# Softmax scales folded into the queries, maximum taken with its sign, relative bias added in place in the bank

## The chip, the core and the metric

The kernel runs on one core of a Trainium2 chip. The metric is the device time of one execution in microseconds, the median of several executions. The core has TensorE (PE: matmuls and transposes), VectorE (DVE), ScalarE (ACT), GpSimd (POOL) and SyncE (SP, which here only issues DMAs). The engines run their own instruction streams and meet at semaphores. Matmul results land in eight banks of PSUM.

## The reference, cut to what matters

Two transformer layers over 256 tokens and 256 context tokens, width 1024. Layer 0 has a gated spatial mixer and a differential attention (four heads, two maps each), then a dense feed-forward network. Layer 1 has a neighbourhood attention with a relative bias (eight heads), a latent attention (four heads), then a mixture of eight experts. The three attentions are what the change touches:

```python
# layer 0: two maps per head, scale = 1/sqrt(64), queries and keys after rope
s = einsum('bqhmd,bkhmd->bhmqk', q, k) * scale
p = einsum('bhmqk,m->bhqk', softmax(s), [1, -lam])
# layer 1, heads of kind C: scale_c = 1/sqrt(64); bias and mask on the 256 local keys only
s_loc = einsum('brqhd,brkhd->bhrqk', qg, kg) * scale_c + bias
s_ctx = einsum('brqhd,bkhd->bhrqk', qg, k_ctx) * scale_c
p = softmax(concatenate([s_loc, s_ctx]))
# layer 1, heads of kind D: scale_d = 1/sqrt(96), no bias
p = softmax(einsum('bqhd,bkhd->bhqk', q, k) * scale_d)
```

## The kernel before

Weights stream through a ring of six 1 MB buffers (`RAW`), each loaded by SP when the one six before it is released, and large matrix products are made of three matmuls over high and low halves. The work runs stage by stage: input products of layer 0 (`run("ev")`), first attention (`att0`), output product, feed-forward, input products of layer 1 (`run_od()`), second attention (`att1`), output product (`odo`), the experts, which fill the second half of the time. Each stage needs the results of the one before.

An attention is a list of units, each one head and 128 queries. `att0` has 16 units with two maps each, 256 keys in eight of them and 512 in the others. `att1` has 16 units of kind C with a bias, then 8 of kind D, all with 512 keys. Each of PE, ACT and DVE walks the list in its own loop, written out in `pe_attention`, `act_attention` and `dve_attention`; the order on an engine is fixed by these loops.

- PE, in step i (L697): scores of unit i+1 into bank 0 or 2 (L691; waits for `exp` of unit i-1), then the four transposes of unit i-1 (L706; wait for `prob` of unit i-1), then, in four steps, a share of the modulation products (`pe_mod_rows`, L571; `pe_mod_turn`, L579), then, for i odd, the product with the values for a pair of units (L717). So the transposes of an even unit are followed by L717, those of an odd unit are not.
- DVE, in step i (L754): the negative row maximum of unit i, then reciprocal (L789) and normalisation (L797, or L792 and L794 for two maps) of unit i-1, which increments `prob`; at odd steps also the low half of a finished pair (L807) or its copy (L804).
- ACT, in step i (L722): the exponentials of unit i with their row sums (L733; wait for `negmax` and for the transposes of unit i-2), the copy of the transposed unit i-1 (L743), at even steps of `att1` the high half of a pair (L750).

For a unit with a bias DVE first waits for the transposes of unit i-2 (L766), since the probabilities of that unit lie in the buffer it will write, and for the bias tile (L767). It then writes the scaled context half (L769) and the scaled local half plus bias (L771) into that SBUF buffer `PB`, and takes the maximum from there (L774). Without a bias, DVE takes the maximum from the bank (L778), waits for itself (`link`), and multiplies it by the scale (L781).

The bias tiles have two buffers. SP (`load_bias`, L941) loads each by two DMAs (L951) once the semaphore `biased` says that the unit two before has used the buffer; POOL then multiplies by the mask and adds the negative infinities (L991, L993) and increments `bias_ready`. The rest of SP's weight loads are queued behind these. The queries come out of the banks by ACT copies: L1033 (s 4 and 5 for layer 0), L1126 (kind C), L1105 (kind D).

Of the kernel before, what the change touches and what calls it, by code (L numbers as in the profile page):

```python
# [23 lines left out]
ALU = mybir.AluOpType  # L24
# [26 lines left out]
NSP_E = 3  # L51
CAP = 128
LAM_INIT = 0.8 - 0.6 * math.exp(-0.3 * 0)

# [109 lines left out]
def trunk(nc, w, out):  # L164
    ctx = ExitStack()
    with ctx:
# [486 lines left out]
        for h in range(4):  # L653
            for qb in range(4):
                nk = 2 if qb < 2 else 4
                att0.append(dict(
                    q=[QK[64 * m:64 * m + 64, h, P * qb:P * qb + P] for m in range(2)],
                    k=[QK[64 * m:64 * m + 64, 4 + h, 0:P * nk] for m in range(2)],
                    nk=nk, scale=1.0 / math.sqrt(64), bias=None, v=[V[:, kt, P * h:P * h + P] for kt in range(nk)],
                    o=slice(0, P), dst=(h, P * qb)))  # L660
        att1 = []
        for h in range(8):
            for qb in range(2):
                p0 = 64 * (h % 2)
                att1.append(dict(
                    q=[QC[p0:p0 + 64, h // 2, P * qb:P * qb + P]], k=[KC[p0:p0 + 64, h // 2, :]],
                    nk=4, scale=1.0 / math.sqrt(64), bias=(h, qb), v=[VCT[:, kt, 64 * h:64 * h + 64] for kt in range(4)],
                    o=slice(p0, p0 + 64), dst=(h // 2, 256 + P * qb)))
        for h in range(4):
            for qb in range(2):  # L670
                att1.append(dict(
                    q=[QD[0:96, h, P * qb:P * qb + P]], k=[KD[0:96, h, :]],
                    nk=4, scale=1.0 / math.sqrt(96), bias=None, v=[VD[:, kt, P * h:P * h + P] for kt in range(4)],
                    o=slice(0, P), dst=(4 + h, 256 + P * qb)))
# [46 lines left out]
        def act_attention(act, a, units, between=lambda i: None):  # L721
            for i in range(len(units) + 3):  # L722
                between(i)
                if i < len(units):
# [5 lines left out]
                    for m in range(len(u["q"])):  # L730
                        src = PB[:, 2 * (i % 2), :n] if u["bias"] else PS[2 * (i % 2) + m][:, :n]
                        c = 8 + 8 * (i % 2) + m
                        last = act.activation(PB[:, 2 * (i % 2) + m, :n], src, ACT.Exp, bias=SM[:, c:c + 1],  # L733
                                              scale=1.0 if u["bias"] else u["scale"],
                                              accum_out=SM[:, c + 2:c + 3])
# [16 lines left out]
        def dve_attention(dve, a, units, between=lambda i: None):  # L752
            lag = 3 + a
            for i in range(len(units) + lag):  # L754
                between(i)
                if i < len(units):
# [7 lines left out]
                    if u["bias"]:  # L764
                        if i >= 2:
                            dve.wait_ge(S(f"ptrans{a}"), i - 1)  # L766
                        dve.wait_ge(S("bias_ready"), i + 1)  # L767
                        b = PB[:, 2 * (i % 2), :]
                        dve.tensor_scalar(b[:, :CTX], PS[2 * (i % 2)][:, :CTX], u["scale"], None, ALU.mult)\  # L769
                           .then_inc(S("biased"), 1)  # L770
                        dve.scalar_tensor_tensor(b[:, CTX:], PS[2 * (i % 2)][:, CTX:], u["scale"], BT[:, i % 2, :],  # L771
                                                 ALU.mult, ALU.add).then_inc(S("biased"), 1)
                        dve.wait_ge(S("biased"), 2 * i + 2)
                        dve.tensor_reduce(SM[:, c:c + 1], b[:, :], AX, ALU.max, negate=True)\  # L774
                           .then_inc(S(f"negmax{a}"), 1)
                    else:
                        for m in range(len(u["q"])):
                            last = dve.tensor_reduce(SM[:, c + 6 + m:c + 7 + m], PS[2 * (i % 2) + m][:, :n], AX,  # L778
                                                     ALU.max, negate=True)
                        link(dve, last)  # L780
                        dve.tensor_scalar(SM[:, c:c + 2], SM[:, c + 6:c + 8], u["scale"], None, ALU.mult)\  # L781
                           .then_inc(S(f"negmax{a}"), 1)
                if 1 <= i <= len(units):
# [101 lines left out]
        def _(sp):  # L885
# [55 lines left out]
            def load_bias():  # L941
                sp.wait_ge(S("n4_hl"), KT)
                for i in range(NB_):
                    h, qb = att1[i]["bias"]
                    if i >= 2:
                        sp.wait_ge(S("biased"), 2 * i - 2)
                    for r in range(2):
# [49 lines left out]
        def _(act):  # L997
# [21 lines left out]
            for g, s in run("ev"):  # L1019
# [3 lines left out]
                for j in range(2):  # L1023
# [8 lines left out]
                    elif s < 8:  # L1032
                        act.activation(QK[:, 2 * (s - 4) + j, :], b[:, :], ACT.Copy).then_inc(S("ev_evac"), 1)  # L1033
                    else:
                        dst = V[:, 2 * j:2 * j + 2, 256 * (s - 8):256 * (s - 7)]
                        act.activation(dst, b[:, :].rearrange("p (t n) -> p t n", t=2), ACT.Copy)\
                           .then_inc(S("ev_evac"), 1)
# [61 lines left out]
            def act_latent(i0, i1):  # L1099

                for i in range(i0, i1):
                    act.wait_ge(S("mla_full"), i + 1)
                    b = PS[2 + i % 2]
                    if i < 4:
                        act.activation(QD[0:96, i, :], b[0:96, :SEQ], ACT.Copy).then_inc(S("mla_evac"), 1)  # L1105
                    elif i < 8:
# [4 lines left out]
            for g, p, s in run_od():  # L1111
# [10 lines left out]
                for j in range(2):  # L1122
                    act.wait_ge(*bank_full(g, j))
                    b = PS[2 + j] if s == 1 else PS[j]
                    if s < 2:
                        act.activation(QC[:, 2 * s + j, :], b[:, :SEQ], ACT.Copy).then_inc(S("od_evac"), 1)  # L1126
                    elif s < 4:
# [836 lines left out]
```

## Time and profile before

| | us |
|---|---|
| median of 3 executions | 2023.33 |
| lowest, highest | 2022.06, 2024.96 |
| the profiled execution | 2020.79 |
| its span in the trace | 2018.6 |
| PE busy | 1908.7 (95%) |
| DVE busy | 1278.3 (63%) |
| ACT busy | 1083.9 (54%) |
| POOL busy | 28.3 (1%) |
| first attention, from its first scores to its last pair | 194 to 245 |
| second attention, kind C | 831 to 893 |
| second attention, kind D | 893 to 917 |

Busy shares are averages over stages with different limits. The granted clock of PE is listed as a share of its higher level. Matmuls are pipelined and the ends in the trace are modelled, so an interval between two starts is safer than a duration. The chain of waits follows the work back from the last instruction, at each step to what released it; its pieces add up to the span.

### The profile page before, as it was taken

To read this page: it belongs to the slowest core of one execution; us is meant where nothing else is said; L and a number is where in the kernel's file an instruction comes from. 1 tells how busy PE (TensorE), PEld (TensorE's weight loads), DVE (VectorE), ACT (ScalarE), POOL (GpSimd) and SP (SyncE) were. 2 spreads that over 40 slices of the span, in tenths; PEclk is the share of its full clock that TensorE was granted. 3 is DMA by queue.
4 is the path that set the end of the run, shared out by engine and by line. 5 is a ranking of instruction groups with operands and counts; after the bars stand their busy time and mean duration, and the time that the engine had idled before them with its cause. 6 is when DMAs were issued, how large, how long until landed. Compare 5 with 4: busy or idle time off the path is not lost.

```text
span 2018.6 us, 23685 instructions
## 1 busy us (share of the span) xinstructions
PE 1908.7 (95%) x9802; PEld 1520.0 (75%) x9802; DVE 1278.3 (63%) x1219; ACT 1083.9 (54%) x1105; POOL 28.3 (1%) x44
## 2 busy tenths in 40 slices
PE   5998798999989989898799999999999999999997
PEld 3886476888878867547688888888888888888886
DVE  2443735222233362363588888888888888888886
ACT  3532535222222263254577676776767767677674
POOL 0000000000000000220000000000000000000000
PEclk9999899999999989899699999999999999999999
DMA  9453063632322271331599998999989999999993
GB/s 316 157 167 125 5 226 113 201 102 86 105 83 88 80 232 35 105 105 61 191 361 364 332 365 327 363 362 333 365 326 366 363 331 365 325 367 359 328 364 145
DMA packets 264229, 473.94 MB, mean 235 GB/s; under 512 B 17145, under 2 KB 116401, under 8 KB 264113
## 3 DMA queue, kind: packets, MB, share of 16 engines
q1 hardware_dynamic: 263216, 469.32, 66.1%
q0 software_dynamic: 896, 3.02, 0.5%
q8 instruction: 80, 1.31, 0.3%
q14 instruction: 37, 0.30, 0.0%
HBM read 471.25 MB, written 1.05 MB: 234 GB/s over the span
## 4 chain that ended last, share of the span: by engine, by line
PE 88%; DVE 5%; ACT 3%; DMA 2%; SPq 1%; issue 1%; DVEq 0%; POOL 0%; ACTq 0%
PE bank L508 26%; PE bank L509 25%; PE bank L510 25%; PE bank L717 2%; PE bank L1826 2%; PE bank L571 1%; DMA raw_weights<-in_w_mod 1%; PE bank L691 1%; PE bank L1864 1%; PE bank L706 1%; SPq L907 1%; PE bank L378 1%; PE bank L365 1%; DVE small L778 1%; ACT split_high L487 1%
## 5 line engine op out<-in xcount | busy, mean ns | idle before, releaser
L1424 DVE TENSOR_TENSOR split_low<-raw_weights,split_high 128x2048 fp32r<-128x2048 f32 x224 | 512.8, 2289 | 61.7 <-ACT split_high L1220 58.2
L1220 ACT ACTIVATE split_high<-raw_weights 128x2048 fp32r<-128x2048 f32 x222 | 426.7, 1922 | 152.7 <-PE bank L510 152.7
L508 PE MATMUL bank<-h_high,split_high 128*128 128x512 f32 (+1 forms) x848 | 325.4, 384 | 22.7 <-DVE h_low L422 9.9
L492 DVE TENSOR_TENSOR split_low<-raw_weights,split_high 128x1024 fp32r<-128x1024 f32 x118 | 143.7, 1225 | 306.5 <-ACT split_high L487 306.4
L509 PE MATMUL bank<-h_low,split_high 128*128 128x512 f32 (+1 forms) x848 | 322.9, 381 | 0.0
L510 PE MATMUL bank<-h_high,split_low 128*128 128x512 f32 (+1 forms) x848 | 322.4, 380 | 0.0
L1424 DVE TENSOR_TENSOR h_low<-raw_weights,h_high 128x2048 fp32r<-128x2048 f32 x112 | 256.7, 2292 | 64.4 <-ACT h_high L1220 64.4
L508 PE MATMUL bank<-split_high,xe_high 128*128 128x512 f32 x672 | 270.4, 402 | 0.0
L510 PE MATMUL bank<-split_high,xe_low 128*128 128x512 f32 x672 | 266.3, 396 | 0.0
L509 PE MATMUL bank<-split_low,xe_high 128*128 128x512 f32 x672 | 266.3, 396 | 0.0
L1220 ACT ACTIVATE h_high<-raw_weights 128x2048 fp32r<-128x2048 f32 x112 | 215.1, 1920 | 58.2 <-PE bank L510 58.2
L487 ACT ACTIVATE split_high<-raw_weights 128x1024 fp32r<-128x1024 f32 x118 | 123.7, 1055 | 194.5 <-PE bank L510 190.3
L508 PEld LDWEIGHTS bank<-h_high,split_high 128*128 128x128 f32 x848 | 163.5, 193 | 56.5 <-issue 17.4
L510 PEld LDWEIGHTS bank<-h_high,split_low 128*128 128x128 f32 x848 | 163.5, 193 | 29.5
L509 PEld LDWEIGHTS bank<-h_low,split_high 128*128 128x128 f32 x848 | 163.6, 193 | 28.5
L510 PEld LDWEIGHTS bank<-split_high,xe_low 128*128 128x128 f32 x672 | 126.7, 189 | 30.5
L509 PEld LDWEIGHTS bank<-split_low,xe_high 128*128 128x128 f32 x672 | 127.0, 189 | 28.7
L508 PEld LDWEIGHTS bank<-split_high,xe_high 128*128 128x128 f32 x672 | 127.0, 189 | 28.7 <-issue 0.3
L508 PE MATMUL bank<-split_high,gt_high 128*128 128x512 f32 x224 | 89.1, 398 | 1.8 <-DVE gt_low L1534 1.8
L510 PE MATMUL bank<-h_high,xe_low 128*128 128x512 f32 x224 | 88.5, 395 | 0.0
L508 PE MATMUL bank<-h_high,xe_high 128*128 128x512 f32 x224 | 88.5, 395 | 0.0
L509 PE MATMUL bank<-split_low,gt_high 128*128 128x512 f32 x224 | 88.5, 395 | 0.0
(248 smaller groups left out, 2550.3 us busy)
## 6 DMA issues: line engine op xcount, KB each, us to landing
raw_weights<-in_moe_w SPq DMA_DIRECT2D x336, 1024.0 KB, 5.8
raw_weights<-in_w_mod SPq DMA_DIRECT2D x48, 1024.0 KB, 5.8
raw_weights<-in_ffn_w SPq DMA_DIRECT2D x33, 1024.0 KB, 5.3
raw_weights<-in_ev_w_in SPq DMA_DIRECT2D x10, 1024.0 KB, 11.8
raw_weights<-in_od_w_in SPq DMA_DIRECT2D x8, 1024.0 KB, 6.8
raw_weights<-in_ev_w_out SPq DMA_DIRECT2D x4, 1024.0 KB, 9.2
raw_weights<-in_od_w_out SPq DMA_DIRECT2D x4, 1024.0 KB, 9.7
overlay<-in_rpb SPq DMA_DIRECT2D x32, 64.0 KB, 2.3
```

Of the source, the lines that this page charges most:

```text
L365: last = pe.matmul(n["sums"](j, t), ones[:, 0:32], n["sq"][:, t % 2, P * j:P * j + P], start=(t == 0 or n["single"]), stop=(t == n["nt"] - ...
L378: last = pe.matmul(dst, ident[0:rows, 32 * j:32 * j + 1].to_broadcast([rows, P]), n["root"][:, c:c + P], start=True, stop=True)
L487: act.activation(half_of(s, j, SPH[:, s % NSPLIT, :]), half_of(s, j, raw_of(r)), ACT.Copy)\
L492: dve.tensor_tensor(half_of(s, j, SPL[:, s % NSPLIT, :]), half_of(s, j, raw_of(split_at[s])), half_of(s, j, SPH[:, s % NSPLIT, :]).bitcast ...
L508: pe.matmul(ps, wh, xh, start=first, stop=False)
L509: pe.matmul(ps, wh, xl, start=False, stop=False)
L510: return pe.matmul(ps, wl, xh, start=False, stop=last)
L571: last = pe.matmul(PS[bank][32 * j:32 * j + 32, 256 * (i % 2):256 * (i % 2) + 256], SC[:, 4 * h + j, :], wt[:, 4 * h + j, :], start=(h == ...
L717: last = pe.matmul(pair_out(units, p)[0], u["v"][kt], PT[p % 2][:, kt, :], start=(kt == 0), stop=(kt == u["nk"] - 1))
L1220: act.activation(esplit(u)[0], RAW[:, u % NRAW, :], ACT.Copy).then_inc(S("e_high"), 1)
L1424: dve.tensor_tensor(lo, RAW[:, u % NRAW, :], hi.bitcast(F32), ALU.subtract).then_inc(S("e_low"), 1)
L1826: last = pe.matmul(PS[XBANK[r]][:, P * f:P * f + P], half[:, t, k:k + P], MP[:, t, e, :], start=(n == 0), stop=(n == 3))
```

## The change

The scale of each attention is applied when ACT copies the queries out of the banks. The products of queries and keys are then already scaled, and the exponentials take no scale. Without a bias the negative maximum goes from the bank straight into the column that the exponential reads; the wait of DVE for itself and the multiplication L781 go. With a bias, DVE adds the bias tile to the local half in the bank, in place, and the maximum and the exponential read the bank; L769 goes, and so does the wait for the transposes of unit i-2. `biased` counts one per unit in place of two.

```diff
+SCALE_B = 1.0 / math.sqrt(64)
+SCALE_C = 1.0 / math.sqrt(64)
+SCALE_D = 1.0 / math.sqrt(96)
...
                     for m in range(len(u["q"])):
-                        src = PB[:, 2 * (i % 2), :n] if u["bias"] else PS[2 * (i % 2) + m][:, :n]
+                        src = PS[2 * (i % 2) + m][:, :n]
                         c = 8 + 8 * (i % 2) + m
                         last = act.activation(PB[:, 2 * (i % 2) + m, :n], src, ACT.Exp, bias=SM[:, c:c + 1],
-                                              scale=1.0 if u["bias"] else u["scale"],
                                               accum_out=SM[:, c + 2:c + 3])
...
                     if u["bias"]:
-                        if i >= 2:
-                            dve.wait_ge(S(f"ptrans{a}"), i - 1)
                         dve.wait_ge(S("bias_ready"), i + 1)
-                        b = PB[:, 2 * (i % 2), :]
-                        dve.tensor_scalar(b[:, :CTX], PS[2 * (i % 2)][:, :CTX], u["scale"], None, ALU.mult)\
-                           .then_inc(S("biased"), 1)
-                        dve.scalar_tensor_tensor(b[:, CTX:], PS[2 * (i % 2)][:, CTX:], u["scale"], BT[:, i % 2, :],
-                                                 ALU.mult, ALU.add).then_inc(S("biased"), 1)
-                        dve.wait_ge(S("biased"), 2 * i + 2)
-                        dve.tensor_reduce(SM[:, c:c + 1], b[:, :], AX, ALU.max, negate=True)\
-                           .then_inc(S(f"negmax{a}"), 1)
-                    else:
-                        for m in range(len(u["q"])):
-                            last = dve.tensor_reduce(SM[:, c + 6 + m:c + 7 + m], PS[2 * (i % 2) + m][:, :n], AX,
-                                                     ALU.max, negate=True)
-                        link(dve, last)
-                        dve.tensor_scalar(SM[:, c:c + 2], SM[:, c + 6:c + 8], u["scale"], None, ALU.mult)\
-                           .then_inc(S(f"negmax{a}"), 1)
+                        local = PS[2 * (i % 2)][:, CTX:]
+                        dve.tensor_tensor(local, local, BT[:, i % 2, :], ALU.add).then_inc(S("biased"), 1)
+                        dve.wait_ge(S("biased"), i + 1)
+                    for m in range(len(u["q"])):
+                        last = dve.tensor_reduce(SM[:, c + m:c + m + 1], PS[2 * (i % 2) + m][:, :n], AX,
+                                                 ALU.max, negate=True)
+                    last.then_inc(S(f"negmax{a}"), 1)
...
                     if i >= 2:
-                        sp.wait_ge(S("biased"), 2 * i - 2)
+                        sp.wait_ge(S("biased"), i - 1)
...
-                        act.activation(QK[:, 2 * (s - 4) + j, :], b[:, :], ACT.Copy).then_inc(S("ev_evac"), 1)
+                        act.activation(QK[:, 2 * (s - 4) + j, :], b[:, :], ACT.Copy, scale=SCALE_B if s < 6 else 1.0)\
+                           .then_inc(S("ev_evac"), 1)
...
-                        act.activation(QD[0:96, i, :], b[0:96, :SEQ], ACT.Copy).then_inc(S("mla_evac"), 1)
+                        act.activation(QD[0:96, i, :], b[0:96, :SEQ], ACT.Copy, scale=SCALE_D).then_inc(S("mla_evac"), 1)
...
-                        act.activation(QC[:, 2 * s + j, :], b[:, :SEQ], ACT.Copy).then_inc(S("od_evac"), 1)
+                        act.activation(QC[:, 2 * s + j, :], b[:, :SEQ], ACT.Copy, scale=SCALE_C)\
+                           .then_inc(S("od_evac"), 1)
```

## Rows read from the trace of the kernel before

**Rows 1.** Stretches 193:248 and 833:890: busy time of PE, PEld, DVE, ACT, POOL, then granted clock.

```profile
193.00:248.00 55.00, 40.52 (x188) 21.82 (x192) 42.09 (x108) 32.01 (x88) 0.00 (x0) 0.84 0.00 1
833.00:890.00 57.00, 48.47 (x207) 22.17 (x206) 34.77 (x81) 24.48 (x53) 22.64 (x32) 0.82 0.24 57
```

**Rows 2.** Waits between 833 and 891 us: us in total, times, longest us.

```profile
DVE y L769 <- PE bank L706: 17.1, 13, 3.3
...
PE bank L706 <- DVE y L797: 5.0, 7, 1.6
```

**Rows 3.** Chain of waits, a pair of kind C: start us, us, what.

```profile
863.11 1.87 PE bank L717 x8
864.98 1.05 PE bank L691 x2
866.03 0.62 PE bank L706 x4
866.88 0.42 DVE y L769
867.30 0.34 DVE y L771
867.67 0.69 DVE small L774
868.46 0.75 DVE y L797
869.25 1.12 PE bank L706 x4
870.37 3.02 PE bank L717 x8
```

**Rows 4.** Timeline, transposes of unit 14; in brackets PE's idle time before.

```profile
890.99 0.66 PE L706 MATMUL bank<-constants,y 128*128 128x128 f32 x4 [1.50 <-DVE y L797]
```

**Rows 5.** One line each: count, shortest/median/longest ns, first and last start, forms.

```profile
L774 DVE TENSOR_REDUCE small<-y x16: 686/686/687, 834.8 to 889.7; 128x1 f32<-128x512 f32 x16
L778 DVE TENSOR_REDUCE small<-bank x40: 412/680/693, 195.4 to 909.8; 128x1 f32<-128x512 f32 x24, 128x1 f32<-128x256 f32 x16
L797 DVE TENSOR_SCALAR y<-y,small x24: 486/488/946, 837.9 to 912.0; 128x512 f32<-128x512 f32 x24
```

**Rows 6.** Stretches of the second attention, columns as in Rows 1.

```profile
836.00:852.00 16.00, 13.47 (x27) 5.79 (x28) 8.39 (x19) 6.60 (x14) 5.97 (x9) 0.50 0.21 43
...
870.00:872.00 2.00, 2.00 (x6) 0.98 (x5) 1.36 (x4) 0.60 (x1) 1.07 (x2) 0.50 0.06 14
```

**Rows 7.** Chain of waits, a unit of kind D.

```profile
904.98 0.70 DVE small L778
905.98 0.50 DVE y L797
906.52 0.66 PE bank L706 x4
```

**Rows 8.** Chain of waits, a unit of the first attention.

```profile
213.24 1.30 DVE small L778 x2
214.56 0.17 DVE small L781
214.73 0.08 DVE small L789
```

**Rows 9.** Timeline, the way of a bias tile, from L771 of unit 6.

```profile
857.09 0.41 DVE L771 SCALAR_TENSOR_TENSOR y<-bank,overlay 128x256 f32<-128x256 f32 x1
...
860.58 0.73 POOL L991 TENSOR_TENSOR overlay<-overlay,constants 128x256 f32<-128x256 f32 x1 [1.18 <-DMA overlay<-in_rpb]
861.39 0.72 POOL L993 TENSOR_TENSOR overlay<-overlay,constants 128x256 f32<-128x256 f32 x1
```

**Rows 10.** The copy of queries and keys of layer 0, and ACT's idle time before it.

```profile
L1033 ACT ACTIVATE overlay<-bank x8: 597/599/599, 107.6 to 153.4; 128x512 f32<-128x512 f32 x8
...
  PE bank L510: 34.4, 8
```

More of the change, by code:

```diff
@@ L658, in trunk @@
                     k=[QK[64 * m:64 * m + 64, 4 + h, 0:P * nk] for m in range(2)],
-                    nk=nk, scale=1.0 / math.sqrt(64), bias=None, v=[V[:, kt, P * h:P * h + P] for kt in range(nk)],
+                    nk=nk, bias=None, v=[V[:, kt, P * h:P * h + P] for kt in range(nk)],
                     o=slice(0, P), dst=(h, P * qb)))
@@ L666, in trunk @@
                     q=[QC[p0:p0 + 64, h // 2, P * qb:P * qb + P]], k=[KC[p0:p0 + 64, h // 2, :]],
-                    nk=4, scale=1.0 / math.sqrt(64), bias=(h, qb), v=[VCT[:, kt, 64 * h:64 * h + 64] for kt in range(4)],
+                    nk=4, bias=(h, qb), v=[VCT[:, kt, 64 * h:64 * h + 64] for kt in range(4)],
                     o=slice(p0, p0 + 64), dst=(h // 2, 256 + P * qb)))
@@ L672, in trunk @@
                     q=[QD[0:96, h, P * qb:P * qb + P]], k=[KD[0:96, h, :]],
-                    nk=4, scale=1.0 / math.sqrt(96), bias=None, v=[VD[:, kt, P * h:P * h + P] for kt in range(4)],
+                    nk=4, bias=None, v=[VD[:, kt, P * h:P * h + P] for kt in range(4)],
                     o=slice(0, P), dst=(4 + h, 256 + P * qb)))
```

## The prediction

> **What bounds the kernel now.** I read the page first: PE is busy nearly everywhere, and more than half of the chain that ends last is the expert products and the feed-forward, which the change doesn't touch. So only the two attentions count, and everything behind them starts when they end: the weight ring is fed by releases that PE itself gives, so a microsecond saved there moves the rest of the program forward by one. The stretches by engine come next [rows 1]. In the second attention PE is busy for 48.5 of 57 us at a mean clock of 0.82, and DVE for 34.8. In the first DVE is busy for 42.1 of 55 us and PE for 40.5. Neither stretch is filled by one engine; the chain of waits has to say who is late.
>
> In kind C the list of waits shows it [rows 2]: DVE waited 13 times, 17.1 us in all, for transposes of the unit two before, and PE's array then waited 7 times, 5.0 us in all, for DVE's normalisation. The chain shows the loop [rows 3]. The transposes of unit 7 end at 866.65. Only then may DVE start unit 9 (L769 at 866.88), since the SBUF buffer has come free; L771, the maximum and the normalisation of unit 8 follow, and PE starts the transposes of unit 8 at 869.25, 2.60 us after those of unit 7 ended. Meanwhile PE has only the scores to do, 1.05 us, so it idles. After an even unit PE also has the product with the values (1.87 us), which covers DVE, and the chain runs on PE alone. So the wait is exposed once in a pair, eight times in 16 units. Where no modulation products stand in between, at units 8 and 14, it is 1.5 us [rows 4]; the other five waits share the remaining 2.0 us, 0.4 each.
>
> **Kind C, what the edit does.** The wait for the transposes goes, and the bank is there earlier: the scores of unit 9 end at 866.03. From there, by the same rows, DVE needs 0.42 for the one remaining 256-wide operation, 0.04 to see its own write, 0.79 from the start of the maximum to the start of the normalisation, 0.50 for that (its median [rows 5]; the row had 0.75) and 0.04 to PE: 1.79, with 0.02 for the start 1.81. So the transposes of unit 8 could start at 867.84 in place of 869.25, 1.41 earlier. PE's own work, transposes and scores, would end at 866.03 + 0.62 + 1.05 = 867.70, so 0.14 us of idle is left. At unit 14 PE was free at 889.49 [rows 4] and by the same count 0.37 is left. In the other pairs modulation products or the low clock keep PE busy longer than 1.81 us, and nothing is left. So 5.0 - 0.14 - 0.37 = 4.5 us. To it comes the head: the first unit waits for its bias tile in either kernel (its maximum starts at 834.8 [rows 5]), but L769 no longer stands between it and its exponential, 0.42 less the small wait kept, about 0.3. Together **4.8 us**. What is late next is PE: 2 x 0.62 of transposes, 1.87 of values and 2 x 1.05 of scores are 5.2 us for a pair [rows 3], before any modulation products.
>
> The operation that reads and writes the bank is not in the trace. L771, which reads a bank and a bias tile and writes SBUF, takes 0.41 us [rows 9]; the maximum over twice as many elements takes 0.69. I take the first, as it has the same inputs, and bound it by nothing added below and 0.27 us above; above counts only where DVE is late, at two pairs fully and in the others within the slack, under 1.5 us in all. The maximum from the bank costs no more than from SBUF: 680 ns against 686 for 512 columns [rows 5]. The Trainium skill ("Perfetto Trace Analysis", section "Optimizing Scalar/DVE Operations") speaks against this part: it gives DVE about 60 ns of access overhead per instruction on SBUF and about 125 on PSUM. By that rule, an estimate, the two operations would be some 0.13 us dearer, and the 4.8 some 0.3 us smaller; the trace shows no such difference for the maximum.
>
> **The clock.** After the long idle before unit 8 the granted clock was 0.50, in 870:872 [rows 6]: the transposes took 1.12 in place of 0.62 us and the values product 3.02 in place of 1.87 [rows 3]. With that idle cut to a tenth I expect PE to stay at 2.4 GHz there: 0.50 + 1.15 = **1.6 us**, between 0 and 1.6. The stretch 836:852 at 0.50 (1.2 GHz) follows the table load and the late bias tile, which stay; I leave it as it is.
>
> **Kind D.** Here DVE already reads the bank and has no wait for transposes. L781 and the wait before it go. From the start of the maximum to the start of the normalisation it took 1.00 us [rows 7], in kind C without L781 0.79 [rows 3]: 0.2 less. The chain passes there three times (units whose transposes aren't covered), so **0.6 us**, at most 8 x 0.2 = 1.6.
>
> **First attention.** Two maxima, L781, reciprocal: reciprocal 1.49 us after the first maximum began [rows 8]. Without L781, with the overlap that kind C shows, it would be 0.19 less. The chain passes L781 nine times, of 16 units, since DVE or the exponential behind it is late there: 9 x 0.19 = **1.7 us**. At the others PE is late (its scores at the low clock), and the gain is zero; the ends are 0.9, if PE takes over in half of the nine, and 16 x 0.19 = 3.0.
>
> **At nothing.** The scale rides on ACT's copies: 4 in each of the three places. The 8 copies of queries and keys take 599 ns each and ACT sat idle 34.4 us before them, waiting for PE [rows 10]; the cover is that idle time, and if a scaled copy took 0.1 us longer it would show in kind D's four at most, where PE waits for them. The exponential reads the bank as it already does in kind D. The bias tile: DVE signals 0.42 us earlier and a tile takes from 857.50 (end of L771) to 862.11 (end of L993), 4.6 us, until it can be used [rows 9]; with 0.5 us of use that is 5.1 us for two units, while the shortest pair I expect is 863.11 to 867.84 and the 0.66 us of transposes, 5.4 us. It is covered with 0.3 us to spare. The loads behind the bias loads on SP's queue start earlier by what the attention gains, and serve the stages after it.
>
> The sum: 4.8 + 1.6 + 0.6 + 1.7 = 8.7 us. The profiled execution took 2020.79 (span 2018.6), so it would be 2012.1. It is 2.5 us under the median of 2023.33, so the median would be **2014.6**.
>
> **Rivals.**
> *A, the next wait is near.* Tile supply has 0.3 us of slack, and the normalisation has a longest case of 946 ns against 488 [rows 5]; POOL's two operations per tile come 3 us after the signal, which with a pair of 5.4 us is just when DVE normalises the next unit. Then the two long stalls keep half of their length (1.3 us) and the clock falls there still (1.6): gain 8.7 - 2.9 = 5.8, and with an add as dear as its upper bound (1.3 more) 4.5: 2018.8. The skill's same section says that GpSimd and DVE share an SBUF read port, which a 2-port operation of DVE holds exclusively; the trace agrees, as L797 alone among these lines has the spread. Against it: L797 had 0.75 in the very stall that was measured, and I counted it as 0.50 only once.
> *B, the clock rises earlier.* In 836:852 PE was busy 13.5 of 16 us at 1.2 GHz [rows 6]. Some of the short stalls go there, so PE is denser. If it is granted 2.4 GHz at half of the stretch, 8 us of work take 4: 12.7 in all, 2010.6.
> *C, the stalls are PE's own.* If the seven waits are put down to DVE wrongly, and PE's pace comes from scores, values and their semaphores, only L781's parts are left, or nothing: 2021 to 2023.3. Against it: the chain passes through DVE by consecutive starts.
> *D, slower.* The place is the same 836:852. The first units come in another rhythm, and if PE, now with the chain of short transposes closer together, is not raised to 2.4 GHz at 852 but stays at 1.2, each microsecond of this costs half of one. It decides from 17 us on (17 / 2 = 8.7), to 869; staying low to the end of kind C at 891 would cost 19.5, and give 2023.3 - 8.7 + 19.5 = 2034. Against it: it rose in the first long run of values and scores, and this run stays whole.
>
> **How the numbers follow.** Forecast 0.58 (2012.3 to 2017.3), A 0.19, B 0.12, C 0.07, D 0.04. The range leaves out C and D: low end from B, 2010.0, high end from A with the executions' own scatter, 2019.8. A measurement of this kernel can tell 0.2%, 4 us, from no change. Faster by more than that: forecast, B and about two thirds of A, 0.58 + 0.12 + 0.12 = 0.82. Same: the rest of A and most of C, 0.14. Slower: D, 0.04.
>
> **What would show it.** Right: in kind C no wait of DVE for L706, waits of PE for L797 of about 0.5 us in all, pairs of 5.4 us where no modulation products stand, clock 1.00 from the end of the first low stretch on; in kind D 0.8 us from maximum to normalisation; in the first attention about 0.19 us less a unit where DVE is late. Wrong: DVE waiting for POOL's L993 beyond the first two units (A), the new add well over 0.42 us, L797 mostly near 0.9 (A), or a second low stretch of the clock in either attention. The prediction fails most easily by the clock, whose part is 1.6 us of the sum and up to 4 us either way.

## The result, and the profile after

The changed kernel took 2005.66 us (median of 4, 2002.99 to 2005.98) against 2022.69 us (median of 4, 2021.35 to 2024.96) for the kernel before: ratio 0.9921, 95% interval 0.9906 to 0.9936. That is 17.0 us less, where 8.7 us were forecast, and the time lies below the stated range. Timed again later the ratio was 0.9942 (0.9923 to 0.9960): 2006.8 us (median of 6) against 2019.93 us, the latter over 29 executions from 2013.15 to 2024.63. The ratio stands for 11.7 us, with an interval from 8.1 to 15.6; the two medians alone differ by 13.1. The executions of one kernel scatter by 11 us, not by the 3 us that the first three showed.

| | before | after |
|---|---|---|
| the profiled execution | 2020.79 | 2005.98 |
| its span | 2018.6 | 2004.1 |
| PE busy | 1908.7 (95%) | 1900.2 (95%) |
| DVE busy, instructions | 1278.3, 1219 | 1269.0, 1179 |
| ACT busy | 1083.9 (54%) | 1081.9 (54%) |

In the changed kernel L769 is the add in the bank, L772 the maximum, L781 the reciprocal, L789 the normalisation, L694 the scores, L709 the transposes, L720 the product with the values, L736 the exponential. First the chain of waits at the pair that [rows 3] showed (units 8 and 9): start us, us, what; the reciprocal and the pieces of 0.02 to 0.04 us called issue are left out.

```profile
857.81 1.87 PE bank L720 x8
859.68 1.07 PE bank L694 x2
860.77 0.44 DVE bank L769
861.24 0.69 DVE small L772
862.03 0.53 DVE y L789
862.61 0.66 PE bank L709 x4
863.27 1.87 PE bank L720 x8
```

DVE now starts 0.02 us after the scores end (860.75), not after the transposes. From the scores' end to the transposes of unit 8 it is 1.86 us; the forecast counted 1.81. The timeline of PE at units 8 and 14, with its idle time in brackets:

```profile
862.61 0.66 PE L709 MATMUL bank<-constants,y 128*128 128x128 f32 x4 [0.24 <-DVE y L789]
...
881.12 0.66 PE L709 MATMUL bank<-constants,y 128*128 128x128 f32 x4 [0.39 <-DVE y L789]
```

The waits between 829 and 882 us (us in total, times, longest):

```profile
DVE bank L769 <- PE bank L694: 16.4, 13, 2.6
DVE bank L769 <- POOL overlay L985: 13.2, 2, 12.9
...
PE bank L709 <- DVE y L789: 0.6, 2, 0.4
```

Forecast were 0.14 and 0.37 us of idle left there, none in the other pairs; the last row has these two waits and no other. DVE waited for PE's scores 13 times, where in [rows 2] it had waited 13 times for the transposes, and for a bias tile only at the first two units. The single lines: count, shortest/median/longest ns, first and last start, forms.

```profile
L769 DVE TENSOR_TENSOR bank<-bank,overlay x16: 411/433/433, 832.1 to 879.3; 128x256 f32<-128x256 f32 x16
...
L772 DVE TENSOR_REDUCE small<-bank x56: 414/691/693, 197.1 to 899.5; 128x1 f32<-128x512 f32 x40, 128x1 f32<-128x256 f32 x16
...
L789 DVE TENSOR_SCALAR y<-y,small x24: 485/488/1019, 835.6 to 901.8; 128x512 f32<-128x512 f32 x24
```

The add that writes the bank takes 433 ns, 18 more than L771 took [rows 9]; the maximum 691 ns, 5 more than L774 [rows 5]. (The median of L771 over its 16 executions is 415 ns.) Kind D and the first attention, chain of waits:

```profile
894.92 0.69 DVE small L772
895.72 0.50 DVE y L789
896.26 0.66 PE bank L709 x4
```

```profile
235.03 1.29 DVE small L772 x2
236.32 0.09 DVE small L781
236.43 0.56 DVE y L784
```

From the maximum to the normalisation of kind D it is 0.80 us, 1.00 before [rows 7]; from the first maximum to the reciprocal in the first attention 1.29, 1.49 before [rows 8]. Both are the 0.2 us of L781 and its wait. The copy of the queries with a scale (now L1025) shows the same duration and the same cover as in [rows 10]:

```profile
L1025 ACT ACTIVATE overlay<-bank x8: 597/599/599, 107.8 to 153.7; 128x512 f32<-128x512 f32 x8
...
  PE bank L513: 34.4, 8
```

**Stages.** Totals scatter too much to show where time goes, so each profile is cut at five starts: first scores and last values product of each attention, first product of the output stage behind the second, and the experts' first dispatch. The starts are those of the lines themselves; for the changed kernel they come from these four rows, the first two in the window of the first attention, the other two in that of the second:

```profile
L694 PE MATMUL bank<-overlay x64: 376/589/1219, 195.8 to 234.4; 64*128 64x256 f32 x32, 64*128 64x512 f32 x32
...
L720 PE MATMUL bank<-y,overlay x48: 379/379/795, 207.0 to 244.5; 128*128 128x256 f32 x48
...
L694 PE MATMUL bank<-overlay x48: 589/595/1219, 829.3 to 898.9; 64*128 64x512 f32 x32, 96*128 96x512 f32 x16
...
L720 PE MATMUL bank<-y,overlay x96: 379/379/689, 844.6 to 906.0; 128*64 128x256 f32 x64, 128*128 128x256 f32 x32
```

| kernel (one profile each), us | to 1st | 1st attention | between | 2nd attention | pause | output stage to dispatch | experts |
|---|---|---|---|---|---|---|---|
| before | 194.0 | 50.3 | 586.9 | 85.3 | 4.6 | 65.7 | 1031.8 |
| before_again | 192.3 | 52.1 | 588.3 | 85.2 | 4.6 | 65.7 | 1031.6 |
| att0_only | 192.1 | 48.8 | 584.6 | 84.8 | 4.7 | 65.6 | 1031.7 |
| d_only | 192.9 | 52.0 | 584.5 | 84.5 | 4.7 | 63.2 | 1031.9 |
| wait_only | 194.9 | 51.8 | 588.1 | 78.5 | 4.7 | 65.7 | 1031.7 |
| c_only | 192.6 | 52.2 | 591.6 | 77.6 | 4.7 | 63.7 | 1031.6 |
| op_only | 193.0 | 48.7 | 587.8 | 80.6 | 4.7 | 63.4 | 1031.5 |
| after | 195.8 | 48.7 | 584.8 | 76.7 | 4.7 | 63.2 | 1030.2 |
| after_again | 193.5 | 48.6 | 588.4 | 76.8 | 4.7 | 63.1 | 1030.6 |
| extra_op | 192.9 | 48.6 | 588.4 | 77.9 | 4.6 | 63.3 | 1031.4 |
| fill_c | 195.4 | 48.6 | 587.4 | 76.6 | 4.6 | 64.4 | 1031.5 |
| delay_before | 191.6 | 52.3 | 588.4 | 84.9 | 6.5 | 63.9 | 1030.0 |
| delay_after | 194.7 | 48.7 | 584.5 | 76.9 | 5.6 | 63.4 | 1031.1 |
| early_split | 194.6 | 48.5 | 588.3 | 76.0 | 1.3 | 61.9 | 1030.9 |

The second attention is steady from one execution to the next, and the first with its fold; the stages between are not. The first took 50.3 to 52.3 us (mean 51.8) in the six profiles without its fold and 48.5 to 48.8 (mean 48.65) in the eight with it: 3.1 us. The second took 85.3 and 85.2 in the kernel before and 76.7, 76.8 (and 76.9 with a delay behind it) in the changed one: 8.5 us. Together 11.6 us, and the ratio timed again gives 0.0058 x 2019.93 = 11.7. So the attentions bring some 11.6 us, and that alone fits the ratio; its interval (8.1 to 15.6 us) would also allow the 2.5 us of the output stage, which is taken up below. The first comparison showed 17.0 because the four executions of before lay at 2021 to 2025. Of the 61 later ones on three chips only 14 reach 2021.35 us, so four in a row are a rare draw, about 1 in 350. Either that is what happened, or the first series ran under other conditions; no run tells.

### The profile page after: what moved, and what is told of

Read it like the earlier page. It is cut to its first block, busy times and chain, and to the rows that moved or that the text cites. A ratio compares the mean times of both kernels' runs of the same rounds, so it can differ in the third digit from the quotient of the medians.

```text
span 2004.1 us, 23645 instructions
## 1 busy us (share of the span) xinstructions
PE 1900.2 (95%) x9802; PEld 1515.2 (76%) x9802; DVE 1269.0 (63%) x1179; ACT 1081.9 (54%) x1105; POOL 28.4 (1%) x44
## 4 chain that ended last, share of the span: by engine, by line
PE 89%; DVE 4%; ACT 3%; DMA 2%; SPq 1%; issue 1%; POOL 0%; DVEq 0%; ACTq 0%
PE bank L511 26%; PE bank L512 26%; PE bank L513 25%; PE bank L720 2%; PE bank L1820 2%; PE bank L574 2%; PE bank L694 2%; DMA raw_weights<-in_w_mod 1%; PE bank L1858 1%; SPq L899 1%; PE bank L709 1%; DVE small L772 1%; PE bank L368 1%; PE bank L381 1%; ACT split_high L490 1%
## 5 line engine op out<-in xcount | busy, mean ns | idle before, releaser
L513 PE MATMUL bank<-h_high,gt_low 128*128 128x512 f32 x224 | 88.5, 395 | 0.0
## 6 DMA issues: line engine op xcount, KB each, us to landing
raw_weights<-in_ev_w_in SPq DMA_DIRECT2D x10, 1024.0 KB, 11.9
```

The source lines that it names most:

```text
L513: return pe.matmul(ps, wl, xh, start=False, stop=last)
```

## The experiments

**The changed kernel again, and its parts.** Two theories stood after the first comparison. Either the attentions carry the whole gain and the untouched stages only differ by how stretches of low clock fall in an execution, or these stages gain each time.

> The changed kernel once more. The profiles of before and after differ by 10.2 us in the two attentions (1.6 and 8.6) and by 4.3 us in stages that the change does not touch, where the stretches of low TensorE clock fell otherwise. Theory 1 (the gain is made in the attentions alone, and the rest is how the low-clock stretches fall in one execution): stage times of this profile scatter by a few us against the first one in the untouched stages, the attentions stay within 2 us of 48.7 and 76.7, and the ratio comes nearer to 0.994 to 0.995. Theory 2 (untouched stages gain each time, since they begin in another rhythm): ratio 0.991 to 0.992 again, untouched stages again shorter by 4 us or more than before.

Measured: 2006.8 us, ratio 0.9942 (0.9923 to 0.9960). Attentions 48.6 and 76.8, within 0.1 us of the first profile; "between" 588.4 against 584.8. The total fits the first theory; the second's 0.991 to 0.992 lies outside the interval.

Only the wait removed: unit i of kind C uses one of four slots of the buffer.

```diff
+        def slot(units, i):
+            return 2 * (i % 2) + (i // 2) % 2 if units[i]["bias"] else 2 * (i % 2)
...
-                        if i >= 2:
-                            dve.wait_ge(S(f"ptrans{a}"), i - 1)
                         dve.wait_ge(S("bias_ready"), i + 1)
-                        b = PB[:, 2 * (i % 2), :]
+                        b = PB[:, slot(units, i), :]
```

> The kernel before, with four SBUF buffers for the scores of kind C in place of two, so that VectorE needs not wait for the transposes of the unit two before; scaling, bias and maximum as before. If the removed wait carries the gain of kind C (my prediction's step): second attention 5 us shorter than 85.3 (path from scores to normalisation 2.24 us, so 0.6 and 0.8 of idle left at units 8 and 14, and the low-clock stretch after unit 8 gone), ratio 0.997 to 0.998. If the removed operation carries it: 1 us or less. If theory 2 holds, 4 us more in untouched stages.

Measured: ratio 0.9974 (0.9963 to 0.9985), 5.3 us; second attention 78.5, 6.8 us shorter where 5 were expected. The idle left at units 8 and 14 is 0.67 and 0.71 us, for the 0.6 and 0.8 expected.

Only the operations removed: the changed kernel with the wait put back.

```diff
+                        if i >= 2:
+                            dve.wait_ge(S(f"ptrans{a}"), i - 1)
                         dve.wait_ge(S("bias_ready"), i + 1)
```

> The changed kernel with VectorE's wait for the transposes of the unit two before put back in kind C. If the wait carries the gain: second attention 2 to 4 us shorter than 85.3 (0.43 us less in each exposed loop of 2.60, seven times, and kind D's 0.6), first attention 1.6 shorter as in the changed kernel, ratio 0.997. If the wait hardly matters: as the changed kernel, second attention at 77.

Measured: ratio 0.9961 (0.9947 to 0.9975), 7.9 us; second attention 80.6, 4.7 us shorter, more than the 2 to 4 expected, first 48.7. The loop through the transposes is exposed again, now without L769 in it. Waits of op_only between 829 and 884 us:

```profile
DVE bank L771 <- PE bank L709: 18.6, 13, 4.0
DVE bank L771 <- POOL overlay L987: 15.5, 3, 12.9
PEld bank L709 <- DVE y L791: 12.4, 11, 1.9
```

Either alone shortens the second attention, by 6.8 and by 4.7 us, and both by 8.6, less than the sum of 11.5: they shorten the same exposed path, and PE is late behind it. A part of each figure is clock (below).

First attention alone, kind C alone, kind D alone:

```diff
-                    nk=nk, scale=1.0 / math.sqrt(64), bias=None, v=[...],
+                    nk=nk, scale=1.0, bias=None, v=[...],
...
+                            o = c + m if a == 0 else c + 6 + m
...
+                        if a == 0:
+                            last.then_inc(S(f"negmax{a}"), 1)
```

> The kernel before with the scale folded into the queries of the first attention alone. My prediction's step: first attention 1.7 us shorter than 50.3 (0.9 to 3.0), second unchanged at 85, ratio 0.999. Theory 2: the later stages are 2 us or more shorter in sum as well, since they all begin at another moment.

Measured: ratio 0.9985 (0.9973 to 0.9997), 3.0 us; first attention 48.8, second 84.8. More than the 1.7 expected, and the traces show why. At the full clock the stage repeats every four units. The maxima of units 7, 11 and 15 start in before_again, which has no low clock between 208.6 and 239.1 us, at

```profile
212.81 1.29 DVE L778 TENSOR_REDUCE small<-bank 128x1 f32<-128x512 f32 x2 [0.34 <-PE bank L691]
...
223.83 1.29 DVE L778 TENSOR_REDUCE small<-bank 128x1 f32<-128x512 f32 x2 [0.34 <-PE bank L691]
...
234.85 1.29 DVE L778 TENSOR_REDUCE small<-bank 128x1 f32<-128x512 f32 x2 [0.34 <-PE bank L691]
```

and in the changed kernel at

```profile
214.18 1.29 DVE L772 TENSOR_REDUCE small<-bank 128x1 f32<-128x512 f32 x2 [0.53 <-PE bank L694]
...
224.61 1.29 DVE L772 TENSOR_REDUCE small<-bank 128x1 f32<-128x512 f32 x2 [0.53 <-PE bank L694]
...
235.03 1.29 DVE L772 TENSOR_REDUCE small<-bank 128x1 f32<-128x512 f32 x2 [0.53 <-PE bank L694]
```

That is 11.02 us for four units without the fold and 10.43 with it, 0.59 less: the 0.2 us count in three units of four, so up to 2.4 us in 16 units. The chain of the kernel before had passed nine units; its profile has two stretches of low clock in mid-stage (217.2 to 220.8 and 227.5 to 231.0 us), in which PE's work takes longer and can hide DVE.

In c_only the diff is that of the change at the lines for a bias, at the queries of kind C and at `load_bias`; d_only is att0_only with `a == 1` and the fold at QD.

> The kernel before with kind C alone as in the changed kernel (scale in its queries, bias added in the bank, maximum and exponential from the bank, no wait for transposes). If kind C carries the second attention's gain: that stage 7.5 to 8 us shorter than 85.3, first attention as before at 50 to 52, ratio 0.995. From output product to dispatch: 63.2 if the clock's low stretches fall by the moment at which that stage starts after kind C's rhythm, 65.7 if what matters is the end of the attention, kind D.

Measured: ratio 0.9963 (0.9949 to 0.9976), 7.5 us; second attention 77.6, 7.7 us shorter.

> The kernel before with the scale of kind D alone folded, so without L781 there. My step: second attention 0.6 us shorter (three exposed units of 0.2), ratio 0.9997. From output product to dispatch 65.7 as before, or, if the end of the attention sets it, 63.2, and then the ratio is 0.9985.

Measured: ratio 0.9998 (0.9989 to 1.0007); second attention 84.5, 0.8 us shorter. The three parts, 3.0, 7.5 and 0.4 us, add up to 10.9, against 11.7 for all of them; within the intervals that is the same.

**What is late in kind C now.** One more VectorE operation where L769 stood:

```diff
+                        dve.tensor_copy(PB[:, 2 * (i % 2) + 1, :CTX], PS[2 * (i % 2)][:, :CTX])
                         local = PS[2 * (i % 2)][:, CTX:]
```

> The changed kernel with one more VectorE operation in each unit of kind C, a 256-wide copy out of the bank into an unused part of the buffer, where L769 stood (0.42 us each, 16 times); the wait for the transposes stays away. If PE is now late in all pairs but two, as I forecast, second attention 0.8 to 1.0 us longer than 76.7 beside what the low-clock stretches do, although 6.7 us of work are added. If VectorE is still the pace of kind C, 5 us or more longer.

Measured: ratio 0.9949 (0.9934 to 0.9964); second attention 77.9, 1.2 us longer for 6.7 us more of DVE's work. PE is the pace in all pairs but two, as forecast: PE's idle time at units 8 and 14 grew from 0.24 and 0.39 to 0.75 and 0.72 us, and with one operation (0.4 us) at the head that is the 1.2.

**The clock.** Mean clock over the whole second attention, the ninth entry after the colon (behind the busy times of PE, PEld, DVE, ACT, POOL), in the order before, after, wait_only, op_only:

```profile
831.00:917.00 86.00, 73.71 (x320) 38.28 (x320) 50.04 (x125) 38.90 (x88) 23.26 (x32) 0.88 0.26 71
```

```profile
829.00:907.00 78.00, 70.49 (x320) 36.94 (x320) 44.13 (x102) 37.56 (x89) 23.42 (x32) 0.91 0.29 78
```

```profile
834.00:914.00 80.00, 70.48 (x321) 36.94 (x320) 50.36 (x125) 38.88 (x88) 23.75 (x32) 0.91 0.28 77
```

```profile
829.00:911.00 82.00, 72.35 (x320) 37.40 (x320) 43.38 (x102) 38.53 (x89) 23.44 (x32) 0.90 0.27 75
```

A clock of 0.88 over 86 us is 10.3 us less of PE's full clock, 0.91 over 78 us 7.0, 0.91 over 80 us 7.2, 0.90 over 82 us 8.2. Taken off the stage times: 75.0, 69.7, 71.3 and 72.4 us. So of the 8.6 us 5.3 are schedule and 3.3 are clock (two digits of the clock leave 0.4 us of doubt in each stage). Counted over quarters of a microsecond, and only while PE was busy, the split is 5.5 and 3.1. In schedule wait_only gained 3.7 and op_only 2.6 us. Both low stretches changed. The one after unit 8 is gone in every kernel that cut either the wait or the operation. The first one lasted 17.2 us in the kernel before (835.0 to 852.2), still 17.3 in op_only, and 13.8 in wait_only, c_only and the changed kernel (832.5 to 846.3), so it became shorter only where the wait was cut. These stretches of the changed kernel stand beside [rows 6]:

```profile
832.00:848.00 16.00, 12.56 (x28) 5.32 (x28) 9.39 (x18) 6.53 (x14) 7.98 (x12) 0.57 0.20 42
848.00:880.00 32.00, 31.76 (x178) 15.51 (x178) 20.02 (x47) 15.48 (x37) 13.97 (x19) 1.00 0.30 74
```

Is the idle time at the head what lowers the clock there? Three extra products fill it:

```diff
             scores(0)
             scores(1)
+            if a == 1:
+                for _ in range(3):
+                    pe.matmul(PS[1][:, :], ident, TAB[:, 0:2, :], start=True, stop=True)
```

> The changed kernel with three extra products (128x512, into a bank not in use) between the scores of unit 1 and of unit 2 of the second attention, where PE waits 4.2 us for the first exponential; they change nothing in the result. The granted clock there fell to 0.50 for 13.7 us, which costs 5.4 us of busy time. If that fall comes from the idle time, it is gone or shorter, and the second attention is 3 to 5.5 us shorter than 76.7. If it comes from something else in the work of kind C (its transposes, the low share of products), it stays, and the stage is 0 to 0.5 us longer.

Measured: ratio 0.9933 (0.9916 to 0.9950), not apart from the changed kernel's; second attention 76.6, against 76.7. The clock stayed at full level through the filled pause. It fell later, 7.0 us after the first scores in place of 3.2, stayed low for 10.5 us in place of 13.8, and that with PE busy throughout:

```profile
831.00:838.00 7.00, 4.98 (x11) 1.98 (x12) 2.49 (x6) 2.65 (x5) 3.05 (x5) 1.00 0.13 28
838.00:850.00 12.00, 12.00 (x28) 5.11 (x27) 6.35 (x13) 4.27 (x11) 7.11 (x10) 0.57 0.20 42
```

From the scores of unit 2 to the end of the first values product the same work took 11.6 us here and 11.9 in the changed kernel. The extra products did not fill the whole pause, as PE's timeline shows; 1.59 us of idle time ended 0.7 us before the fall at 838.4:

```profile
833.32 2.84 PE L702 MATMUL bank<-angles,constants 128*128 128x512 f32 x6
837.75 1.28 PE L694 MATMUL bank<-overlay 64*128 64x512 f32 x2 [1.59 <-ACT y L739]
```

In early_split, below, only 0.90 us was left, PE was busy again from 836.14 on, and the clock fell at 838.4 all the same. So to fill most of the pause moves the fall but doesn't prevent it; whether the idle time that remains causes it, or the work of kind C, stays open. The low stretch covers the first units, which are scores and transposes only, and ended in fill_c and in the changed kernel during the first product with the values.

**The stage behind the attention.** Three early profiles without, and three with, the scale folded in the second attention gave 65.7 and 63.2 us from output product to dispatch, though nothing there is changed.

> The kernel before once more, for its profile. From the start of the output product to the experts' dispatch the three kernels with scaled queries in the second attention took 63.1 to 63.4 us, the three without 65.6 to 65.7. If the change has a systematic part there, this profile has 65.7 again. If it is only how the low-clock stretches fall in an execution, it can be either. The second attention should be within 2 us of 85.3, the first within 2 of 50.3.

Measured: 65.7 again, attentions 52.1 and 85.2. The single time, 2022.05, says nothing more.

The two delays are extra ScalarE copies between the second attention and the first weight split behind it (one for delay_after, both for delay_before):

```diff
             act_table(act, ACT.Sqrt, 50)
+            act.activation(YEH[:, :], TAB[:, :, :].rearrange("p a n -> p (a n)"), ACT.Copy)
+            act.activation(XEH[:, :, :].rearrange("p a n -> p (a n)"), TAB[:, :, :].rearrange("p a n -> p (a n)"), ACT.Copy)
             for g, s in run("odo"):
```

> The kernel before with two extra ScalarE copies (128x1024, about 1.0 us each, into tiles not in use yet) between the second attention and the first split of the output product's weights, so a pause of about 2.1 us more. Over the kernels so far the clock fell 0.7 to 0.9 us before the first output product where output product to dispatch took 65.7 us, and later than 0.3 us before it where it took 63.2. If the moment is what counts, the pause is 6.7 in place of 4.6 and the stage behind it can change by 2.4 us either way. If the edit itself made the stage shorter, it stays at 65.7 and the whole is 2.1 us slower.

Measured: ratio 1.0006 (0.9996 to 1.0016). In the profile the pause is 6.5 us, 1.9 longer, and the stage behind it took 63.9, 1.8 shorter. The times of ten executions allow from 0.8 us less to 3.2 us more, so they can't tell a delay that cost nothing from one that cost its 1.9 us.

> The changed kernel with one such copy, a pause of about 1.0 us more. If the moment is what counts, the output product starts 1.0 us later against the fall of the clock, which then comes 0.3 to 0.6 us before it, and output product to dispatch goes to 65.7 or part of the way, the whole 1 to 3.5 us slower. If the edit itself made the stage shorter, it stays at 63.2 and the whole is 1.0 us slower.

Measured: ratio 0.9941 (0.9926 to 0.9957), as without the delay, though 1.0 us lies within the interval; pause 5.6, stage 63.4, which did not go back to 65.7. The clock fell 0.2 us before the first output product here, so the fall had not come where the stages of 65.7 us have it.

The stage takes 65.6 to 65.7 or 63.1 to 64.4 us in kernels that are identical there; d_only and c_only, too, have it at 63.2 and 63.7, with one of the edits each, and delay_before has 63.9 with none. It goes with the clock: in the four profiles with 65.6 or 65.7 us the clock fell 0.7 to 0.9 us before the first output product and stayed low for 6.8 us. In delay_before it stayed low as long, but 2.3 us of that lay in the pause; the 1.6 us more at half the clock explain 0.8 of the 1.8 us, and the rest stays open. In the others it fell later and stayed low for 3.4 us. (early_split is left out here, as its stage begins with less work to do.) The stretch at the start of the stage in the kernel before, and in the changed one:

```profile
920.00:928.00 8.00, 6.87 (x35) 6.90 (x36) 4.40 (x5) 3.89 (x5) 0.00 (x0) 0.57 0.61 201
```

```profile
910.00:918.00 8.00, 7.33 (x49) 7.36 (x50) 5.16 (x5) 3.45 (x5) 0.00 (x0) 0.79 0.70 217
```

So the stage's time goes with where the low stretch lies, read from one profile of each kernel; that the start of the stage sets this isn't shown, as delay_after didn't move it. Nor is it shown that it favours the changed kernel in the mean: the ratio of d_only is 0.9998 although its profile has the short stage, where a gain of 2.5 us in each execution would have given 0.9984, outside its interval.

**A version meant to beat both.** Two fill products, the table for the exponential loaded ahead of the wait, and the first split of the output stage's weights inside kind C:

```diff
+            act_table(act, ACT.Exp, 54)
             act_attention(act, 1, att1, mods_between)
...
+                if i in (5, 11):
+                    to(of["odo"][0], i // 11)      # ScalarE
...
+                if i in (6, 12):
+                    to(of["odo"][0], i // 12)      # VectorE
```

> A version meant to beat both: the changed kernel with two of these extra products, ScalarE's table for the exponential loaded before it waits for the first maximum, and the first weights of the output product split into halves inside kind C (ScalarE at steps 5 and 11, VectorE at 6 and 12) in place of after the attention. By the traces: table 1.28 us off the head, 3 to 4 of the 4.7 us between attention and output product, and what the clock gives. Ratio against the kernel before 0.989 to 0.992, against the changed one 4 to 9 us.

Measured: 2001.05 us, ratio 0.9906 (0.9889 to 0.9923), 16.6 us less than the 2017.67 of the kernel before beside it (19.0 by the ratio); the changed kernel was 13.1 us less in its own repeat (11.7 by the ratio). It beats the kernel before clearly. Against the changed kernel, which was not timed beside it, the intervals of the ratios touch at 0.9923; in the profiles the stages from the second attention to the dispatch are 5.4 us shorter. The pause behind the attention is 1.3 us in place of 4.7, the second attention 0.7 us shorter, where the table's 1.28 had been expected and more from the clock. What each of the three edits brings was not run apart.

## Why the prediction was right in kind and wrong in size

- **What bounds kind C, the exposed wait.** Right. The loop through the transposes was on the path; without it the path from scores to transposes is 1.86 us (1.81 forecast), the idle left at units 8 and 14 is 0.24 and 0.39 us (0.14 and 0.37), and nothing is left elsewhere. In schedule alone the second attention gained 5.3 us where kind C's 4.8 and kind D's 0.6 had been summed. In parts it fits too: with the clock's share taken off by quarters of a microsecond, c_only gained 4.8 and d_only 0.7 us. wait_only and op_only show that wait and operation shorten one path.
- **The add in the bank.** Right: 433 ns for the 0.42 us assumed. The Trainium skill's overhead for PSUM ("Perfetto Trace Analysis", section "Optimizing Scalar/DVE Operations") would have had some 130 ns more over the two operations; 18 and 5 ns were measured.
- **The clock in the second attention.** A mis-sized term: 1.6 us forecast, 3.3 measured. The low stretch after unit 8 went as forecast. The one at the head was left "as it is", and became 3.4 us shorter (835.0 to 852.2 before, 832.5 to 846.3 after), worth 1.7 us. Rival B had the mechanism, with twice its size.
- **Kind D.** Right: 0.2 us an exposed unit, 0.8 us in d_only for the 0.6.
- **First attention.** The second mis-sized term: 1.7 us forecast from nine passages of the chain, 3.1 in the mean of the stage times and 3.0 by the ratio of att0_only, at the upper bound of 3.0. The step's unit price was right (1.49 to 1.29 us). Its count was low: at the full clock it is three units of four, up to 2.4 us, and not nine of 16, which is what the chain shows in a profile with low stretches. For the rest, 0.7 us or more, the clock is the only difference the traces show, and the prediction put it at nothing in this stage: summed over the stage, one less the granted clock comes to 8.2 to 10.8 us (mean 9.7) in the six profiles without the fold and 7.2 to 7.6 in the eight with it. One pair of profiles showed 1.6 us, since the kernel before had its shortest first attention of six there.
- **At nothing.** Right: the scaled copies take the same 599 ns under the same cover, and no unit beyond the second waited for its tile. L789's longest case was 1019 ns. In the second attention of both kernels the normalisation took 0.48 to 0.49 us whenever POOL's two operations on a bias tile didn't run at the same time; all longer cases, up to 1.02 us, overlap them. In the changed kernel these mostly fell where PE had other work to do.
- **The sum against the median.** Wrong, and this made the largest part of the miss. 2014.6 was 2023.33 less 8.7, so three executions were taken as the kernel's level. They lay high: the medians of 29, 11 and 21 later executions of the same kernel are 2019.93, 2017.67 and 2019.12. The high end of the range took the executions' scatter as about 1 us (2018.8 to 2019.8), when executions of either kernel spread over 7 to 11. Of the 8.9 us between 2014.6 and 2005.66, 3.4 are this base (2023.33 - 2019.93), 2.9 the two terms above (11.6 - 8.7), and the rest, 2.6, is not accounted for: the four executions after lay 1.1 us under their own repeat, and stages that weren't touched differed too. The 8.7 us themselves lie inside the repeat's 8.1 to 15.6; 17.0 came out because that first series had its kernel before at 2022.69, for a reason that stays open.
- **Rivals.** A didn't come: no wait for tiles. C is refuted by wait_only, 5.3 us for the wait alone. D, the clock staying low longer, went the other way (its 17 / 2 is 8.5, not 8.7, which changes nothing).

## What to carry to other kernels

Read in the chain which buffer or bank the first operation of a loop waits for; a wait that guards only a buffer can be removed by not using that buffer, and what that brings is the time from the earlier event, worked out until the next engine is late. Stages with many short waits on TensorE also lose to the clock, and a shorter path gives that back as well, so such a term needs a range of its own on both sides. Count the exposed passages in a stretch without low clock, since a low clock hides some of them. Before a sum is set against a median, look how far executions of that kernel spread; three close values don't show it, and the times of a stage that the change touches are steadier across profiles than totals.

## What the runs showed of the hardware

- Executions of one kernel on one core spread over 11 us (2013.15 to 2024.63), while the attentions repeat within 0.1 to 0.3 us in the changed kernel. The spread goes with the clock: the shortest of these had a mean granted clock of 0.971, the longest 0.964. In the profiles it lies in stages whose work is the same, with low-clock stretches at other places ("between" from 584.5 to 591.6 us).
- In one profile a pause 1.9 us longer came with a stage 1.8 us shorter behind it (delay_before); more of a low stretch of the same 6.8 us lay in the pause.
- With most of a pause filled, PE's clock fell later and then stayed at 0.50 for 10.5 us in which PE was busy throughout, on scores (64 rows), transposes and the first product with the values (fill_c).
- VectorE's normalisation (fp32, 128x512) took 0.48 to 0.49 us alone and up to 1.02 us while GpSimd worked on a bias tile.
